# First norm of a two-layer mixer kernel: turned in chunks of two tiles, its gain applied as columns

## The chip, the cores and the metric

One core of one Trainium2 chip. The metric is the device time of one execution in microseconds, the median of several runs. TensorE multiplies and turns (transposes), VectorE (DVE in the rows), ScalarE (ACT) and GpSimd (POOL) compute, SyncE (SP) issues most DMAs. All data is fp32.

## The reference

Two layers of three mixers (difference attention, latent attention, cross attention to a memory), each followed by a two-matrix MLP, and then a third block of another kind. Only the first lines matter here; `x` is 512 rows by 1024 columns:

```python
def rmsnorm(x, gain):
    y = x * lax.rsqrt(jnp.mean(x * x, axis=-1, keepdims=True) + EPS)
    return y * gain
for l in range(DEPTH):
    h = rmsnorm(x, g_mix[l])
    dq, dk, dv, c_q, c_kv_kr, xq, gate_logits = jnp.split(h @ w_in[l], split_idx, axis=-1)
```

The program computes `c_q` (384 columns) first and `c_kv_kr` (288 columns) second, then the others.

## The kernel before, in words

Rows are cut into four tiles of 128 (t = 0 to 3), the 1024 columns of `h` into eight chunks of 128 (k = 0 to 7). For a product the rows of `h` are turned, so that each chunk lies on the partitions: `h_T_hi` and `h_T_lo` hold the turned `h` as a high part in the rounded matmul format and the rest. Weights are split in the same way: a unit of 256 weight rows (two chunks) is loaded by a DMA of SyncE, ScalarE writes the high part (L361, "weights_high_r"), VectorE the low part (L368, "weights_r"). Every product is three matmuls: high by high (L427), high by low (L428), low by high (L429).

Each engine runs its own list in order, and a wait in the list holds everything behind it. The lists are made by a planner: each stage gets times in units of one step of the products (`P_.at`, `P_.beside`), and each engine takes the steps of all stages in order of these times, at equal times in order of entry. TensorE can have a later time for a step than the others (the third entry of `at`).

The first section, cq, has four units of weights and two passes, tiles 0 and 1 and then tiles 2 and 3: a step is one unit by one tile, six matmuls of 384 columns. So cq is plan times 0 to 15, and ckv, matmuls of 288 columns, is 16 to 31. `Tokens.act` and `Tokens.dve` split the weights ahead of use: at cq's step 0 up to the fourth unit, at 2 the fifth, at 4 the sixth. Six units fit in the weight buffer.

The first norm is `StartNorm` (L894). Before: the vector g_mix is loaded broadcast over all partitions (512 KB, SyncE), the squares (L934, ScalarE) wait for the identity too, VectorE multiplies x by the gain (L990), takes the inverse roots of two tiles' sums (`Root`, L703 to L720) and scales tile 0 (L972), ScalarE scales tile 1 (L956). TensorE turns both (L919, 16 turns of 128x128), ScalarE copies out the high part (L942, 512 columns at a time) and VectorE the low part (L980). Tiles 2 and 3 follow with one operation for scale and gain (L1010). The first weight loads wait until x tile 1 has landed (`sp.wait_ge("x_in", 1)`). All four high parts and all four low parts of tiles 0 and 1 come before the first product.

Around it stand the tables of sines and cosines: `TableTurns` (L1654 to L1667, the whole turns), `TableRest` (L1686 to L1695) and `TableSines` (L1712 on ScalarE, L1723 on VectorE), then `Gains` (L1740 to L1767, scaling of small vectors), and `LatentNorm` of cq (squares L1178, scaling L1193), whose turned rows (L632) are used later. cq and ckv are written to a ring of two PSUM banks ("gemm 2": banks 0 and 1) and copied out by ScalarE (L581).

Of the kernel before, what the change touches and what calls it, by code (L numbers as in the profile page):

```python
# [15 lines left out]
P = 128  # L16
# [369 lines left out]
class Tokens(Stage):  # L386
# [3 lines left out]
    def __init__(self, c, tag, xT, chunks, src, sink, ready=(), tiles=NT, ring="gemm", together=NT, tile_ready=lambda t: ()):  # L390
        self.c, self.tag, self.xT, self.chunks, self.sink, self.ready, self.tiles = c, tag, xT, chunks, sink, ready, tiles
        self.ring, self.cols, self.tile_ready = ring, src.shape[1], tile_ready
# [11 lines left out]
    def pe(self):  # L404
# [489 lines left out]
class StartNorm(TileNorm):  # L894


    n = 6
# [4 lines left out]
    def tile_scaled(self, t, g, lane):  # L902
        self.c.values[("scaled", self.tag, t, g)] = lane.end

    def sp(self):
        sp = self.c.sp
        sp.wait_ge("x_in", 1)
        self.c.stream.sp(0)
        for _ in range(self.n):
            yield  # L910

    def pe_turn(self, t):
        c, pe = self.c, self.c.pe
        for g in range(2):
            pe.wait_ge("scaled", self.tag, t, g)
            bank = c.fill(self.tag, t, g, ring=self.ring)
            for k in range(4):
                at = (4 * g + k) * P
                mm = pe.e.transpose(bank[:, k * P:(k + 1) * P], self.xg[:, t, at:at + P], c.ident[:, :])  # L919
            mm.then_inc(*pe.tell("filled", self.tag, t, g))  # L920

    def pe(self):
        for pair in ((), (), (0, 1), (), (2,), (3,)):
            for t in pair:
                self.pe_turn(t)
            yield
# [10 lines left out]
    def act_high(self, t):  # L937
        c, ac = self.c, self.c.ac
        for g in range(2):
            ac.wait_ge("filled", self.tag, t, g)  # L940
            ac.wait_all(self.free)
            ac.e.activation(self.tile(c.hT_all[0], t, g), self.got(t, g), ACT.Copy).then_inc(*ac.tell("turned_high", self.tag, t, g))  # L942

    def act(self):
# [3 lines left out]
        for t in range(2):  # L948
            self.act_squares(t)
        yield  # L950
        c.stream.act(1)
        for g in range(2):
            xg = self.halves(self.xg[:, 1, :])[g]
            ac.wait_ge("gained", self.tag, 1, g)
            ac.wait_ge("inverse_root", self.roots[0].tag)
            ac.e.activation(xg, xg, ACT.Copy, scale=self.sums[0][:, 1:2]).then_inc(*ac.tell("scaled_act", self.tag, g))  # L956
            self.tile_scaled(1, g, ac)
        yield
        for t in range(2):
            self.act_high(t)  # L960
        for t in range(2, NT):
            self.act_squares(t)
        yield
        yield
        for t in range(2, NT):
            self.act_high(t)
            yield

    def dve_scale(self, t, g):
        ve, xg = self.c.ve, self.halves(self.xg[:, t, :])[g]  # L970
        ve.wait_ge("gained", self.tag, t, g)
        ve.e.tensor_scalar(xg, xg, self.sums[0][:, t:t + 1], None, ALU.mult).then_inc(*ve.tell("scaled_dve", self.tag, t, g))  # L972
        self.tile_scaled(t, g, ve)

    def dve_low(self, t):
        c, ve = self.c, self.c.ve
        for g in range(2):
            ve.wait_ge("turned_high", self.tag, t, g)
            ve.wait_all(self.free)
            ve.e.tensor_tensor(self.tile(c.hT_all[1], t, g), self.got(t, g), self.tile(c.hT_all[0], t, g).bitcast(F32),  # L980
                               ALU.subtract).then_inc(*ve.frees(self.tag, t, g))

    def dve(self):
        c, ve = self.c, self.c.ve
        ve.wait_all(self.gain_in)
        for t in range(2):
            for h in range(2):
                x, gain, xg = (self.halves(y)[h] for y in (c.x[:, t, :], self.gain, self.xg[:, t, :]))
                ve.wait_all(self.x_ready(t, h))
                ve.e.tensor_tensor(xg, x, gain, ALU.mult).then_inc(*ve.tell("gained", self.tag, t, h))  # L990
        for h in range(2):
            ve.wait_ge("tile_squares", self.tag, 1, h)
        self.roots[0].dve()
        for g in range(2):
            self.dve_scale(0, g)
        yield
        c.stream.dve(1)
        yield
        for t in range(2):
            self.dve_low(t)  # L1000
        c.stream.dve(3)
        yield
        for h in range(2):
            ve.wait_ge("tile_squares", self.tag, NT - 1, h)
        self.roots[2].dve()
        for t in range(2, NT):
            for g in range(2):
                x, gain, xg = (self.halves(y)[g] for y in (c.x[:, t, :], self.gain, self.xg[:, t, :]))
                ve.wait_all(self.x_ready(t, g))
                ve.e.scalar_tensor_tensor(xg, x, self.sums[0][:, t:t + 1], gain, ALU.mult, ALU.mult).then_inc(*ve.tell("gained", self.tag, t, g))  # L1010
                self.tile_scaled(t, g, ve)
        yield
        for t in range(2, NT):
            self.dve_low(t)
            yield

# [627 lines left out]
class TableTurns(Stage):  # L1644
# [7 lines left out]
    def dve(self):  # L1652
        c, ve, t_ = self.t.c, self.t.c.ve, self.t
        ve.e.memset(c.stat[:, 0:1], 0.0).then_inc(*ve.tell("zero"))  # L1654
# [125 lines left out]
class Layer1:  # L1780
# [3 lines left out]
    def __init__(self, c, l, plan, start, x_marks, hT_free, norm_times):  # L1784
# [44 lines left out]
        if l == 0:  # L1829
            tables = Tables(c, ((self.cos_d, self.sin_d), (self.cos_r, self.sin_r)), [("in", "positions")])  # L1830
            P_.at(Load(c, "identity", [(c.ident[:, :], i["identity"])], []), (-2.9,))
            P_.at(Load(c, "positions", [(c.pos_i[:, :], i["positions"]),
                                        (tables.freq, i["inv_freq"][0, :].partition_broadcast(P))], [], True), (-3,))
        norm_cells = wide_norm_cells(c)
        gain_load = Load(c, tag("g_mix"), [(norm_cells[0], i["g_mix"][l].partition_broadcast(P))], hT_free if l else [])
        P_.at(gain_load, (norm_times[0][0] - 1,))
        norm_of = (c, tag("norm"), x_marks, norm_cells[0], [("in", tag("g_mix"))], *norm_cells[1:], wide(A, NT), hT_free, hT_free)
# [4 lines left out]
        def section(name, dst, col, n, free, ring="gemm 2"):  # L1842
            return Tokens(c, tag(name), c.hT, KD, w[:, col:col + n], CopyOut(c, lambda t: dst[t][:, 0:n], free, by="act"),
                          ring=ring, together=2, tile_ready=norm.done)
# [8 lines left out]
        cq_job, ckv_job = section("cq", cq, C_CQ, MQ, x_gone), section("ckv", ckv, C_CKV, MKV + MR, x_gone)  # L1853
# [2294 lines left out]
class Program:  # L4148


    def __init__(self, c, out):
        self.c = c
        self.plan = plan = Plan()
        both = lambda t, h: [("x_in", t), ("in", "identity")]
        start, hT_free, x_marks = [], [("in", "identity")], both
        for l in range(DEPTH):
            plan.begin()
            times = (tile_times(-16, 4, 4.8),) if l else ((-0.9, -0.8, -0.7, 0.1, 5.8, 5.9),)
# [27 lines left out]
def build(nc, ins, out):  # L4186
# [30 lines left out]
    c.pos_i = sb("positions_int", [P, NT], I32)  # L4217
# [56 lines left out]
def laid_out(inputs):  # L4274
    packed = [name for name, n in (*ROWS_1, *COLUMNS_1, *ROWS_2, *COLUMNS_2)]
    arrays = {name: a for name, a in inputs.items() if name not in packed}
    arrays["positions"] = inputs["positions"].reshape(NT, P).T
    arrays["vectors_1"] = np.stack([vectors(inputs, l, ROWS_1, COLUMNS_1) for l in range(DEPTH)])
# [15 lines left out]
```

## Time and profile before

| what | value |
|---|---|
| median of 3 runs | 3432.21 us (3430.88 to 3433.6) |
| the profiled execution | 3431.43 us |
| its span | 3429.9 us |
| mean granted clock of TensorE | 0.992 |
| TensorE busy | 3310.9 us, 97% |
| VectorE, ScalarE busy | 2018.7 us (59%), 1354.2 us (39%) |

The span is the time between the first and the last record of the profile; 1.5 us of the execution lie around it. The granted clock is 1.00 for 2.4 GHz and 0.50 for 1.2 GHz.

### The profile page before, as it was taken

Reading aid. Unit: us, or ns where it says so; the run is one execution under the profiler, and the core shown is the slowest. Engines: PE = TensorE matmul, PEld = TensorE weight load, DVE = VectorE, ACT = ScalarE, POOL = GpSimd, SP = SyncE. Lnnn points to the kernel's source line nnn. Section 1 sums busy time; section 2 is a strip of 40 time slices with the busy share of each in tenths; the row PEclk is TensorE's granted clock in tenths of the full one; section 3 lists DMA queues with packets and bytes.
Section 4 is the critical chain, followed back from the end, with each engine's and each line's share of the span. In section 5 each row is a group of like instructions: output and inputs, shape, how many; then the busy total and the mean of one; then the engine's idle time right before and its main releaser. Section 6 shows DMA issues by size and latency. Waiting matters only on the chain.

```text
span 3429.9 us, 53077 instructions
## 1 busy us (share of the span) xinstructions
PE 3310.9 (97%) x21864; PEld 2720.9 (79%) x21864; DVE 2018.7 (59%) x3803; ACT 1354.2 (39%) x2604; POOL 0.2 (0%) x4
## 2 busy tenths in 40 slices
PE   7989999999999999999999999999999999999998
PEld 7777788888888777788888888777777788888887
DVE  6776753554436776753554438775766678664434
ACT  5456543342225466543343224434443324232222
POOL 0000000000000000000000000000000000000000
PEclk9999999999999999999999999999999999999999
DMA  4221223233324221223233334333411235433332
GB/s 141 80 70 50 56 74 105 92 99 98 98 99 127 86 64 50 57 79 105 86 105 99 96 101 118 89 92 106 125 38 40 92 95 157 135 97 94 97 98 86
DMA packets 353875, 315.31 MB, mean 92 GB/s; under 512 B 10288, under 2 KB 281776, under 8 KB 353636
## 3 DMA queue, kind: packets, MB, share of 16 engines
q1 hardware_dynamic: 352916, 309.75, 29.9%
q8 instruction: 175, 2.87, 0.3%
q10 hardware_dynamic: 720, 2.16, 0.2%
q14 instruction: 64, 0.52, 0.0%
HBM read 288.28 MB, written 23.59 MB: 91 GB/s over the span
## 4 chain that ended last, share of the span: by engine, by line
PE 80%; DVE 11%; ACT 5%; issue 3%; DMA 2%; SPq 0%; DVEq 0%; ACTq 0%
PE banks L532 14%; PE banks L534 13%; PE banks L533 13%; PE banks L427 8%; PE banks L429 8%; PE banks L428 8%; DVE weights_r L368 2%; PE banks L632 1%; ACT weights_high_r L361 1%; PE banks L2928 1%; PE banks L2867 1%; PE banks L1241 1%; PE banks L1228 1%; PE banks L1332 1%; PE banks L2881 1%
## 5 line engine op out<-in xcount | busy, mean ns | idle before, releaser
L368 DVE TENSOR_TENSOR weights_r<-weights,weights_high_r 128x1024 fp32r<-128x1024 f32 (+2 forms) x517 | 592.9, 1154 | 355.7 <-ACT weights_high_r L361 354.6
L532 PE MATMUL banks<-h_T_hi,weights_high_r 128*128 128x512 f32 (+2 forms) x1912 | 759.6, 397 | 10.6 <-DVE h_T_lo L881 4.7
L534 PE MATMUL banks<-h_T_hi,weights_r 128*128 128x512 f32 (+2 forms) x1912 | 737.9, 386 | 0.0
L533 PE MATMUL banks<-h_T_lo,weights_high_r 128*128 128x512 f32 (+2 forms) x1912 | 737.5, 386 | 0.0
L361 ACT ACTIVATE weights_high_r<-weights 128x1024 fp32r<-128x1024 f32 (+2 forms) x517 | 511.2, 1000 | 360.8 <-DMA weights<-in_w_mlp 213.3
L532 PEld LDWEIGHTS banks<-h_T_hi,weights_high_r 128*128 128x128 f32 x1912 | 361.4, 189 | 98.6 <-issue 28.8
L534 PEld LDWEIGHTS banks<-h_T_hi,weights_r 128*128 128x128 f32 x1912 | 361.2, 189 | 72.7
L533 PEld LDWEIGHTS banks<-h_T_lo,weights_high_r 128*128 128x128 f32 x1912 | 361.7, 189 | 68.0 <-issue 2.6
L427 PE MATMUL banks<-weights_high_r,h_T_hi 128*128 128x512 f32 (+2 forms) x672 | 279.3, 416 | 9.2 <-DVE gate L2208 3.7
L429 PE MATMUL banks<-weights_high_r,h_T_lo 128*128 128x512 f32 (+2 forms) x672 | 254.9, 379 | 0.0
L428 PE MATMUL banks<-weights_r,h_T_hi 128*128 128x512 f32 (+2 forms) x672 | 254.7, 379 | 0.0
L602 DVE TENSOR_TENSOR cellsX<-cellsX,banks 128x512 f32<-128x512 f32 x112 | 76.7, 685 | 276.3 <-PE banks L429 276.2
L427 PE MATMUL banks<-weights_high_r,cellsM_r 128*128 128x512 f32 (+1 forms) x464 | 181.6, 391 | 0.0
L428 PE MATMUL banks<-weights_r,cellsM_r 128*128 128x512 f32 (+1 forms) x464 | 178.1, 384 | 0.0
L429 PE MATMUL banks<-weights_high_r,cellsC_r 128*128 128x512 f32 x432 | 169.2, 392 | 0.0
L427 PEld LDWEIGHTS banks<-weights_high_r,h_T_hi 128*128 128x128 f32 x672 | 127.6, 190 | 41.3 <-issue 9.7
L427 PE MATMUL banks<-weights_high_r,cellsE_r 128*128 128x512 f32 x384 | 150.3, 391 | 2.4 <-DVE cellsS L3898 2.4
L428 PE MATMUL banks<-weights_r,cellsE_r 128*128 128x512 f32 x384 | 150.0, 391 | 0.0
L429 PE MATMUL banks<-weights_high_r,cellsB_r 128*128 128x512 f32 x384 | 149.6, 390 | 0.0
L428 PEld LDWEIGHTS banks<-weights_r,h_T_hi 128*128 128x128 f32 x672 | 128.0, 190 | 23.2 <-issue 3.9
L429 PEld LDWEIGHTS banks<-weights_high_r,h_T_lo 128*128 128x128 f32 x672 | 127.5, 190 | 22.9
L1541 DVE TENSOR_TENSOR gate<-gate,banks 128x512 f32<-128x512 f32 x64 | 44.0, 687 | 131.2 <-ACT gate L1533 131.2
(562 smaller groups left out, 5228.5 us busy)
## 6 DMA issues: line engine op xcount, KB each, us to landing
weights<-in_w_in SPq DMA_DIRECT2D x183, 512.0 KB, 3.8
weights<-in_w_mlp SPq DMA_DIRECT2D x128, 512.0 KB, 3.8
weights<-in_ffn_w_in SPq DMA_DIRECT2D x44, 512.0 KB, 3.8
weights<-in_w_out SPq DMA_DIRECT2D x24, 512.0 KB, 3.6
weights<-in_ffn_w_down SPq DMA_DIRECT2D x22, 512.0 KB, 3.5
weights<-in_w_mem_kv SPq DMA_DIRECT2D x16, 512.0 KB, 3.5
weights<-in_w_diff_o SPq DMA_DIRECT2D x16, 512.0 KB, 3.6
weights<-in_w_mla_o SPq DMA_DIRECT2D x8, 512.0 KB, 3.4
```

The costliest lines, as they stand in the source:

```text
L361: ac.e.activation(self.part(c.w_high_r, u), self.part(c.w_raw, u), ACT.Copy).then_inc(*ac.tell("high", u))
L368: ve.e.tensor_tensor(self.part(c.w_raw_r, u), self.part(c.w_raw, u), self.part(c.w_high_r, u).bitcast(F32), ALU.subtract).then_inc(*ve.tel ...
L427: pe.e.matmul(out, lhsT=hi[k][:, tok], rhs=wh[:, j, :], start=(k == 0), stop=False)
L428: pe.e.matmul(out, lhsT=hi[k][:, tok], rhs=wl[:, j, :], start=False, stop=False)
L429: mm = pe.e.matmul(out, lhsT=lo[k][:, tok], rhs=wh[:, j, :], start=False, stop=last)
L532: pe.e.matmul(out, lhsT=wh[:, k, :], rhs=hi[k][:, cols], start=(k == 0), stop=False)
L533: pe.e.matmul(out, lhsT=wh[:, k, :], rhs=lo[k][:, cols], start=False, stop=False)
L534: mm = pe.e.matmul(out, lhsT=wl[:, k, :], rhs=hi[k][:, cols], start=False, stop=(k == self.chunks - 1))
L602: ve.e.tensor_tensor(dst, dst, got, ALU.add).then_inc(*ve.frees(*key))
L632: mm = pe.e.transpose(bank[0:m, at:at + rows], src, c.ident[0:rows, 0:rows])
L1228: mm = pe.e.matmul(bank[:, 0:v[j].shape[-1]], lhsT=c.pT[n % 2][:, j * P:(j + 1) * P], rhs=v[j], start=(j == 0), stop=(j == len(v) - 1))
L1541: ve.e.tensor_tensor(y, y, got, ALU.mult).then_inc(*ve.frees(*key))
```

## The change

The vector arrives as eight columns (128 partitions by 8) instead of a broadcast row, and is multiplied in after the turn, in the copies out of PSUM, where a chunk's columns of `h` lie on the partitions. The identity is the first load of SyncE's queue and the columns the second; the six first weight loads follow at once, and then positions and frequencies, vectors and mem. x tiles still come on ScalarE's queue. The squares no longer wait for the identity. After the turn of two chunks of two tiles (a bank), the first product may start: `chunk_ready` is a new wait of `Tokens`. Between its wait for the identity and its wait for the scaled rows TensorE turns the identity 28 times into the first bank. cq and ckv of the first layer use the ring of four banks. The tables and the gains have later times.

```diff
 class Tokens(Stage):
             if first:
                 pe.wait_ge("low", u)
+                for k in range(part):
+                    pe.wait_all(self.chunk_ready(n, k0[u] + k))
 class StartNorm(TileNorm):
     def sp(self):
-        sp.wait_ge("x_in", 1)
         self.c.stream.sp(0)
+    def pe_turn(self, pair, b):
+        first = pair == b == 0
+        if first:
+            bank = c.fill(self.tag, pair, b, ring=self.ring)
+            for _ in range(28):
+                pe.e.transpose(bank[:, 0:P], c.ident[:, :], c.ident[:, :])
+        for t in (2 * pair, 2 * pair + 1):
+            pe.wait_ge("scaled", self.tag, t, b // 2)
+        if not first:
+            bank = c.fill(self.tag, pair, b, ring=self.ring)
+        for k in range(2):
+            at = (2 * b + k) * P
+            for t in range(2):
+                mm = pe.e.transpose(bank[:, (2 * k + t) * P:(2 * k + t + 1) * P], self.xg[:, 2 * pair + t, at:at + P], c.ident[:, :])
+        mm.then_inc(*pe.tell("filled", self.tag, pair, b))
     def pe(self):
-        for pair in ((), (), (0, 1), (), (2,), (3,)):
+        self.c.pe.wait_ge("in", "identity")
+        for pair in range(2):
+            for b in range(4):
+                self.pe_turn(pair, b)
+                yield
+    def act_high(self, pair, b):
+        for k in range(2):
+            f = 2 * b + k
+            ac.e.activation(c.hT[0][f][:, self.cols(pair)], self.got(pair, b, k), ACT.Copy, scale=c.first_gain[:, f:f + 1])
     def act(self):
         for t in range(2):
             self.act_squares(t)
         c.stream.act(1)
+        self.act_scale(1)
+        self.act_high(0, 0)
+        c.stream.act(2)
+        yield
+        self.act_high(0, 1)
+        self.act_squares(2)
+        c.stream.act(3)
+        self.act_squares(3)
+        yield
+        self.act_high(0, 2)
+        c.stream.act(4)
+        yield
+        self.act_high(0, 3)
+        self.act_scale(3)
+        yield
+        for b in range(4):
+            self.act_high(1, b)
+            yield
+    def dve_low(self, pair, b):
+        for k in range(2):
+            f = 2 * b + k
+            ve.e.scalar_tensor_tensor(c.hT[1][f][:, self.cols(pair)], self.got(pair, b, k), c.first_gain[:, f:f + 1],
+                                      c.hT[0][f][:, self.cols(pair)].bitcast(F32), ALU.mult, ALU.subtract)
     def dve(self):
-                ve.e.tensor_tensor(xg, x, gain, ALU.mult)
+        ve.e.memset(c.stat[:, 0:1], 0.0)
+        self.dve_root(0)
+        self.dve_scale(0)
+        c.stream.dve(1)
+        self.dve_low(0, 0)
+        yield
+        for b in range(1, 4):
+            c.stream.dve(b + 1)
+            if b == 2:
+                self.dve_root(2)
+            self.dve_low(0, b)
+            if b == 2:
+                self.dve_scale(2)
+            yield
+        for b in range(4):
+            self.dve_low(1, b)
+            yield
+    def chunk_done(self, pair, k):
+        return [("emptied", self.tag, pair, k // 2)]
 class Layer1:
+            P_.at(Load(c, "first columns", [(c.first_gain, i["g_mix_columns"])], []), (-2.8,))
-            P_.at(Load(c, "positions", ...), (-3,))
+            P_.at(Load(c, "positions", ...), (0.5,))
-        cq_job, ckv_job = section("cq", ...), section("ckv", ...)
+        cq_job, ckv_job = section("cq", ..., "gemm 2" if l else "gemm", **({} if l else {"chunk_ready": norm.chunk_done})), section("ckv", ..., "gemm 2" if l else "gemm")
-            P_.at(tables.whole, (-1.5,))
-            P_.at(tables.rest, (6.2,))
-            P_.at(tables.sines, (11.6, 13.6))
-        P_.beside(Gains(c, l, self, vectors_in), 15, 18)
+            P_.at(tables.whole, (5.7,))
+            P_.at(tables.rest, (7.8,))
+            P_.at(tables.sines, (16.3, 16.6))
+        P_.beside(Gains(c, l, self, vectors_in), 15 if l else 17.5, 18 if l else 20.5)
 class Program:
-            times = ... ((-0.9, -0.8, -0.7, 0.1, 5.8, 5.9),)
+            times = ... ((-0.9, -0.8, 1.5, 3.5, 5.5, 5.6, 7.6, 7.7), [0, 0, 0, 0, 0.9, 1, 1.9, 3.8])
```

`act_scale` is the scaling that L956 did, straight from x and for tiles 1 and 3; `dve_scale` the same on VectorE for tiles 0 and 2; `dve_root` waits for the squares of two tiles and takes their inverse roots. The numbers in `times` are the plan times of the norm's eight steps, the list behind them what TensorE's are later by.

## Rows read from the trace of the kernel before

**Rows 1.** The page: the chain that ended last, by engine.

```profile
PE 80%; DVE 11%; ACT 5%; issue 3%; DMA 2%; SPq 0%; DVEq 0%; ACTq 0%
```

**Rows 2.** Waits of TensorE, whole span: us in total, times, longest.

```profile
PE banks L919 <- DVE cellsA L972: 17.6, 1, 17.6
PE banks L427 <- DVE weights_r L368: 1.9, 1, 1.9
```

**Rows 3.** Timeline until the first turn: start us, us, engine, line, what [idle before].

```profile
8.13 3.06 SPq L381 DMA_DIRECT2D weights<-in_w_in  x6
9.29 0.63 ACT L934 ACTIVATE cellsS<-cellsX 128x512 f32<-128x512 f32 x1 [4.15 <-DMA identity<-in_identity]
12.44 2.50 DVE L990 TENSOR_TENSOR cellsA<-cellsX,cellsS 128x512 f32<-128x512 f32 x4 [2.29 <-DMA cellsS<-in_g_mix]
13.78 0.84 ACT L361 ACTIVATE weights_high_r<-weights 128x768 fp32r<-128x768 f32 x1 [1.93 <-DMA weights<-in_w_in]
15.07 0.16 DVE L703 TENSOR_TENSOR tile_sums<-tile_sums 128x2 f32<-128x2 f32 x1
17.05 0.88 DVE L972 TENSOR_SCALAR cellsA<-cellsA,tile_sums 128x512 f32<-128x512 f32 x2
17.11 1.34 ACT L956 ACTIVATE cellsA<-cellsA,tile_sums 128x512 f32<-128x512 f32 x2 [2.48 <-DVE tile_sums L720]
17.59 3.68 PE L919 MATMUL banks<-identity,cellsA 128*128 128x128 f32 x16 [17.59 <-DVE cellsA L972]
```

**Rows 4.** DMA issues in stretches 0.7:0.75, 1.16:1.18, 8.1:8.2: KB, us to landing.

```profile
cellsX<-in_x ACTq DMA_DIRECT2D x1, 512.0 KB, 4.1
positions_int<-in_positions SPq DMA_DIRECT2D x1, 2.0 KB, 3.3
...
cellsX<-in_x ACTq DMA_DIRECT2D x1, 512.0 KB, 7.0
...
weights<-in_w_in SPq DMA_DIRECT2D x1, 384.0 KB, 5.6
```

**Rows 5.** Busy time by stretch: PE, PEld, DVE, ACT, POOL, clock, DMA share, GB/s.

```profile
0.00:10.00 10.00, 0.00 (x0) 0.00 (x0) 2.63 (x10) 2.20 (x5) 0.20 (x4) 1.00 0.70 235
10.00:17.50 7.50, 0.00 (x0) 0.00 (x0) 4.73 (x17) 3.08 (x9) 0.00 (x0) 1.00 1.06 383
26.00:32.00 6.00, 5.87 (x25) 5.84 (x26) 5.52 (x17) 1.70 (x3) 0.00 (x0) 0.72 0.00 1
```

**Rows 6.** Timeline of the first sections, all engines.

```profile
23.00 0.33 PE L427 MATMUL banks<-weights_high_r,h_T_hi 128*128 128x384 f32 x1
26.13 0.61 PE L427 MATMUL banks<-weights_high_r,h_T_hi 128*128 128x384 f32 x1 [1.90 <-DVE weights_r L368]
31.99 1.91 PE L919 MATMUL banks<-identity,cellsA 128*128 128x128 f32 x16
33.66 0.42 PE L427 MATMUL banks<-weights_high_r,h_T_hi 128*128 128x384 f32 x1
36.43 0.96 DVE L1686 SCALAR_TENSOR_TENSOR probabilities<-probabilities 128x768 f32<-128x768 f32 x1
40.20 0.56 DVE L1695 TENSOR_SCALAR probabilities<-probabilities 128x768 f32<-128x768 f32 x1
44.15 0.29 PE L427 MATMUL banks<-weights_high_r,h_T_hi 128*128 128x288 f32 x1
53.62 1.41 DVE L1193 TENSOR_SCALAR cellsX<-cellsX,small 128x384 f32<-128x384 f32 x4
55.17 0.63 PE L632 MATMUL banks<-identity,cellsX 128*128 128x128 f32 x4 [0.22 <-DVE cellsX L1193]
```

**Rows 7.** Groups by line and form in 0:60: busy us, mean ns.

```profile
L368 DVE TENSOR_TENSOR weights_r<-weights,weights_high_r 128x768 fp32r<-128x768 f32 x4 | 3.6, 952 | 2.5 <-ACT weights_high_r L361 2.5
L643 ACT ACTIVATE cellsM_r<-banks,small 128x512 fp32r<-128x512 f32 x3 | 2.1, 687 | 4.9 <-PE banks L632 4.9
L1767 DVE TENSOR_TENSOR small<-small 128x256 f32<-128x256 f32 x2 | 0.8, 418 | 0.0
```

More of the change, by code:

```diff
@@ L386, with __init__ @@
 class Tokens(Stage):
-    def __init__(self, c, tag, xT, chunks, src, sink, ready=(), tiles=NT, ring="gemm", together=NT, tile_ready=lambda t: ()):
+    def __init__(self, c, tag, xT, chunks, src, sink, ready=(), tiles=NT, ring="gemm", together=NT, tile_ready=lambda t: (), chunk_ready=lambda n, k: ()):
         self.c, self.tag, self.xT, self.chunks, self.sink, self.ready, self.tiles = c, tag, xT, chunks, sink, ready, tiles
+        self.chunk_ready = chunk_ready
         self.ring, self.cols, self.tile_ready = ring, src.shape[1], tile_ready
@@ L894 @@
 class StartNorm(TileNorm):
-    n = 6
+    n = 8
     def __init__(self, c, tag, *args):
         super().__init__(c, tag, *args, pairs=True)
-    def tile_scaled(self, t, g, lane):
-        self.c.values[("scaled", self.tag, t, g)] = lane.end
     def sp(self):
-        sp = self.c.sp
-        sp.wait_ge("x_in", 1)
         self.c.stream.sp(0)
@@ L910, in sp, with cols, got @@
             yield
-    def pe_turn(self, t):
-        c, pe = self.c, self.c.pe
[L914 to L920, printed above, removed]
-    def pe(self):
-        for pair in ((), (), (0, 1), (), (2,), (3,)):
-            for t in pair:
-                self.pe_turn(t)
-            yield
+    def cols(self, pair):
+        return slice(2 * pair * P, 2 * (pair + 1) * P)
+    def got(self, pair, b, k):
+        return self.c.slots[(self.tag, pair, b)][:, k * 2 * P:(k + 1) * 2 * P]
+    def pe_turn(self, pair, b):
+        c, pe = self.c, self.c.pe
+        first = pair == b == 0
[12 more added lines that the diff above has]
+        mm.then_inc(*pe.tell("filled", self.tag, pair, b))
+    def pe(self):
+        self.c.pe.wait_ge("in", "identity")
[3 more added lines that the diff above has]
+                yield
     def act_squares(self, t):
@@ L935, in act_squares, with act_scale @@
                             accum_out=self.sums[h][:, t:t + 1]).then_inc(*ac.tell("tile_squares", self.tag, t, h))
-    def act_high(self, t):
+    def act_scale(self, t):
         c, ac = self.c, self.c.ac
+        ac.wait_ge("inverse_root", self.roots[t - 1].tag)
         for g in range(2):
-            ac.wait_ge("filled", self.tag, t, g)
-            ac.wait_all(self.free)
-            ac.e.activation(self.tile(c.hT_all[0], t, g), self.got(t, g), ACT.Copy).then_inc(*ac.tell("turned_high", self.tag, t, g))
+            ac.e.activation(self.halves(self.xg[:, t, :])[g], self.halves(c.x[:, t, :])[g], ACT.Copy,
+                            scale=self.sums[0][:, t:t + 1]).then_inc(*ac.tell("scaled_act", self.tag, t, g))
+            c.values[("scaled", self.tag, t, g)] = ac.end
+    def act_high(self, pair, b):
+        c, ac = self.c, self.c.ac
+        ac.wait_ge("filled", self.tag, pair, b)
+        ac.wait_all(self.gain_in)
+        ac.wait_all(self.free)
+        for k in range(2):
+            f = 2 * b + k
+            ac.e.activation(c.hT[0][f][:, self.cols(pair)], self.got(pair, b, k), ACT.Copy, scale=c.first_gain[:, f:f + 1]).then_inc(
+                *(ac.tell("turned_high", self.tag, pair, b) if k else ac.step()))
     def act(self):
@@ L949, in act @@
             self.act_squares(t)
+        c.stream.act(1)
+        self.act_scale(1)
+        self.act_high(0, 0)
+        c.stream.act(2)
         yield
[L951 to L957, printed above, removed]
+        self.act_high(0, 1)
@@ L975, in dve_low, with dve_scale @@
-    def dve_low(self, t):
+    def dve_scale(self, t):
         c, ve = self.c, self.c.ve
         for g in range(2):
[L978 to L981, printed above, removed]
+            ve.e.tensor_scalar(self.halves(self.xg[:, t, :])[g], self.halves(c.x[:, t, :])[g], self.sums[0][:, t:t + 1], None,
+                               ALU.mult).then_inc(*ve.tell("scaled_dve", self.tag, t, g))
+            c.values[("scaled", self.tag, t, g)] = ve.end
@@ L983, in dve, with dve_root @@
+    def dve_root(self, t):
+        ve = self.c.ve
+        for h in range(2):
+            ve.wait_ge("tile_squares", self.tag, t + 1, h)
+        self.roots[t].dve()
     def dve(self):
         c, ve = self.c, self.c.ve
[L985 to L995, printed above, removed]
-        yield
[L997 to L1011, printed above, removed]
@@ L1018, with done, x_gone @@
+        for b in range(4):
[3 more added lines that the diff above has]
+        return [("emptied", self.tag, pair, k // 2)]
+    def done(self, t=None):
+        return [("emptied", self.tag, pair, b) for pair in (range(2) if t is None else (t // 2,)) for b in range(4)]
+    def x_gone(self):
+        return [("tile_squares", self.tag, NT - 1, 1), ("scaled", self.tag, NT - 1, 1), ("scaled", self.tag, NT - 2, 1)]
 class FinalNorm(Stage):
```

48 lines of the change are left out of this document (22 added, 26 removed).

## The prediction

> **What bounds the kernel.** I read the page first: the chain that ended last is TensorE for 80% [rows 1]. So the end moves by what TensorE gains or loses, and only where it stands still or runs slowly. The waits of TensorE come second: one of them, 17.6 us until the first turned rows, is more than twice any other, and the change goes for it; the 1.9 us until the second unit of weights lies in the same stretch [rows 2]. Third, the timeline says what made up the 17.6 us [rows 3]. The squares stood until the identity was there (9.29). The multiply by the gain stood until the broadcast vector was there (12.44) and four of them took 2.5 us. Then came the root, 15.07 to 17.05, the scaling, and the first turn at 17.59. Fourth, from there to ckv's first product at 44.15 [rows 6] are 26.6 us. They hold 96 products of cq, which go at 0.173 us when fast (60 of them lie between 33.66 and 44.15, 10.5 us), and 32 turns at 0.115 us (16 in 1.9): 16.6 + 3.7 = 20.3 us. The other 6.3 us are low clock and the 1.9 us wait. All that can be had is therefore some 6 us there and some 6 us of the 17.6.
>
> **Part 1, the start.** Times are from the start of the profiled span.
>
> x tile 1 landed at 1.17 + 7.0 = 8.2 [rows 4]. The gain broadcast, positions and frequencies no longer share the engines ahead of it, but weights do. Bounds are 7.2 and 9.4 (the last if weights take half of the 2.35 MB that had moved by 10 us [rows 5]); I take 7.8, near the row. Its squares: eight halves and roots are paced 0.61 us, so two take 1.3 (9.29 to about 11.9 for four [rows 3]): 9.1. Root 2.0 us: 11.1. VectorE scales tile 0 by 12.0 (0.88 for two).
>
> ScalarE however has the first unit of weights between the squares and the scaling of tile 1. That unit landed at 8.13 + 5.6 = 13.7 [rows 4]. Its issue no longer waits for x tile 1 and falls at about 1.6. Before it or beside it go x (2.1 MB), the unit (0.39) and identity and columns (0.07), together 2.56 MB; 2.35 MB had moved by 10 us and the rate was then 0.383 MB per us [rows 5], so it lands at 10.6. Bounds: 9.0 (if x3 comes after it) and 13.7 as before. Split 0.84, first half of tile 1 scaled in 0.67 (1.34 for two) [rows 3]: first turn of rows at **12.2**, for 17.59, with bounds 11.7 (root) and 15.3.
>
> The 28 turns of the identity go on TensorE ahead of that. Positions, as first of SyncE's queue, landed at 4.0 and x tile 0 at 4.8 [rows 4], so I take 4.5 for the identity. At the slow pace, 0.23 us each (16 in 3.68 [rows 3]), they take 6.4 us and end at 10.9; at 0.115 they take 3.2. They cost nothing while they end before 12.2.
>
> **Part 2, cq.** Prices first. A high part of two chunks is two ScalarE operations of 256 columns with a scale. The row of that kind has 512 columns and 0.69 us [rows 7]; 256 must lie between half of it and all of it, I take 0.40 each and 0.72 for a pair at pace. A low part is two VectorE operations of 256, of which a plain one is 0.42 [rows 7]: 0.85 for a pair (0.7 to 1.5). The unit's split is 0.75 on ScalarE at pace and 0.95 on VectorE.
>
> ScalarE, in list order from 12.95 (first bank filled): high 0, unit 2, high 1, two squares 1.25, unit 3, two squares 1.25, unit 4, then high 2: it starts at 19.0. VectorE: low 0 at 13.7, over at 14.5; low 1 over at 16.2; then units 3 and 4, the last until 20.0 as it waits for ScalarE; then the root of tiles 2 and 3, 2.0 us; then low 2, over at **22.8**. TensorE: first two banks, stands from 13.2 to 14.5, 12 products to 16.6, third bank, 12 products to 19.1, fourth bank to 19.6, and then it stands **3.2 us** for low 2. This wait takes the place of the old 1.9 us one; queued behind the root on VectorE are low 2, the scaling of tile 2 and both later low parts, and TensorE waits for each. After it the clock is at its lower level for 3.4 us (after the 1.9 us wait the stretch 26 to 32 had a mean of 0.72, that is 0.28 x 6 / 0.5 [rows 5]), which costs some 1.6 us, partly hidden. From 22.8: unit 3 to 26.4, then one step, two banks, one step to 29.4, low part of pair 1 at 29.7, then 48 products 8.3 and two banks 0.9: ckv starts at **38.9**, for 44.15, so 5.2 us earlier. If TensorE comes slowly out of the start, the 3.2 us wait shrinks by as much; that term hardly moves (4.8 to 6.2 with the clock low or high at each place).
>
> Four banks for two: the copies of a pass no longer stand before the next. The rows show 10.49 us for what 60 products at 0.173 do in 10.38 [rows 6], so 0.1 us at most for cq. I take 0.
>
> **Part 3, what is late next.** The rest of the tables took VectorE from 36.43 to 40.76, ahead of ckv, and it then had idle time. Now it stands behind the last low part, which TensorE fills only after two units of the second pass: over about 2.3 us before ckv, so the tables' rest (4.35 us) ends 2.1 us after ckv's start. From there to the scaled cq rows VectorE has units 0.7 + 0.7, sines 0.45, the two parts of Gains 0.9 + 1.7, two units 2.4, the root 1.8, the scaling 1.4 (53.62 to 55.03 [rows 6]), with gaps 10.4 us: ready 12.6 us after ckv's start. TensorE wanted them 10.8 us after it (55.17 less the 0.22 wait [rows 6], less 44.15). So it stands 1.8 us where it stood 0.2: **1.6 us lost**. Whether the clock falls there too is open; one chance in three at 1.6 us, in the sum as 0.4. The whole tables (2.9 us) lie between low 1 and low 2 of pair 1, while TensorE does 12 products; hidden. Later times and orders are as before, VectorE idles 1.5 us and more behind that point, and everything moves by the same amount.
>
> Sum: 5.2 - 1.6 - 0.4 = 3.2; the other way round of the clock in the first stretch adds 0.3 on average: **3.5 us**. The profiled execution is 3431.4 (span 3429.9), so 3427.9 against it; the median is 0.8 above the profiled one. Prediction 3428.7.
>
> **A rule that speaks against it.** At 17.59 the turns go at 0.23 us and products follow at the slow pace until 23.0, which is 3.5 us of turns and 1.7 us of products; after the wait at 26.13 products alone ran slowly for 3.4 us [rows 3, 5, 6]. So here turns seem to have counted towards the rise of the clock. The Trainium skill, page "TensorE: Matmul & The Clock Gate", Part 4 on PE-mode transpose, says that turns do not count as busy for the clock. By it the 28 turns would buy nothing; this trace speaks rather against it but has no stretch of turns alone.
>
> **Rivals.**
> 1. The identity's turns warm nothing, so the change does not do what it says there. Then banks 0 and 1 take 0.46 us longer each and the first 12 products run at 0.32 for 0.173, 2.7 us in all; the wait for low 2 takes up most of it, as VectorE's list moves only by 0.5. Gain 3.0 us: 3429.2. For it: no rows of turns alone. Chance 0.25, in the same class as the forecast.
> 2. Faster: the rise holds and there is no wait at low 2 (VectorE's root comes early enough as ScalarE runs ahead of my list). Then ckv starts at 14.5 + 16.6 + 2.8 = 33.9, 10.2 us earlier, less 1.7 at the cq turns: 8.5 us, 3423.7. Against it: five ScalarE operations and a root in the list order that I counted from rows. With the parts between (no fall of the clock at either wait, an earlier unit of weights) 0.2 for more than 6.9 us.
> 3. Slower: the filler stands in the way. TensorE's list is in order. If the identity lands where it did before, at 9.2 (its squares waited for it until 9.29 [rows 3]), 28 slow turns end at 15.7, rows begin 3.5 us later and the gain to ckv is 1.7. With 1.6 lost at the cq turns and 1.6 of clock there the end is 1.5 us later: 3433.7. It decides from an identity at 5.8 on. Against it: now it is first in its queue. Chance 0.1; over 0.2% slower would need 5 us more.
> 4. VectorE is the bound to the cq turns and the gain is given back there, since its list holds 2 us more than TensorE's time. Gain 0 to 1.5: 3431.5. Chance 0.15.
>
> **Numbers.** Forecast 0.3, rivals 0.25, 0.2, 0.1, 0.15. A measurement of this kernel can tell about 0.2% from no change, 6.9 us, so most cases are "same". Faster 0.2, same 0.78, slower 0.02. The range 3423.5 to 3433 takes in rival 2 at its end and most of rival 3, with the bounds of the unit's landing (3 us).
>
> **What would show it.** Right: first row turn near 12.2; a wait of TensorE for the low part of the third bank near 3 us; ckv's first product near 39; the first cq turn near 51.6 with a wait of 1 to 2 us. Wrong: no wait at the third bank; the identity's turns still running when rows are scaled; rows' turns at 0.115 us from the start with products fast at once, or at 0.23 us after 28 turns (rival 1); a ckv start under 36 or over 42.

## The result, and the profile after

The changed kernel is slower: 3445.6 us median (10 runs, 3439.6 to 3451.1) against 3437.0 before (10 runs, 3430.9 to 3443.4), ratio 1.0028, interval 1.0018 to 1.0037. Forecast was 3428.7 in a range of 3423.5 to 3433. In a second comparison on another occasion the ratio was 1.0022 (1.0013 to 1.0031). The three runs of before known at the time lay in the lower half of its spread. Single executions of the unchanged kernel differ by more than the loss (3430.9 to 3443.4 in these ten), so all that follows goes by medians, intervals, and stretches of the trace.

The start went as foreseen, and better up to ckv. The page of the profile (the chain that ended last) and the timeline of the changed kernel, columns as in [rows 3]:

```profile
PE 80%; DVE 10%; ACT 5%; issue 3%; DMA 1%; SPq 0%; DVEq 0%; ACTq 0%
...
4.07 5.37 PE L922 MATMUL banks<-identity 128*128 128x128 f32 x28 [4.07 <-DMA identity<-in_identity]
5.90 0.63 ACT L946 ACTIVATE cellsS<-cellsX 128x512 f32<-128x512 f32 x1
9.25 0.84 ACT L361 ACTIVATE weights_high_r<-weights 128x768 fp32r<-128x768 f32 x1 [2.02 <-DMA weights<-in_w_in]
10.85 1.06 PE L930 MATMUL banks<-identity,cellsA 128*128 128x128 f32 x8 [1.41 <-ACT cellsA L953]
13.41 0.41 PE L430 MATMUL banks<-weights_high_r,h_T_hi 128*128 128x384 f32 x1 [1.50 <-DVE h_T_lo L1007]
21.85 0.48 PE L430 MATMUL banks<-weights_high_r,h_T_hi 128*128 128x384 f32 x1 [3.14 <-DVE h_T_lo L1007]
22.13 0.52 PE L431 MATMUL banks<-weights_r,h_T_hi 128*128 128x384 f32 x1
38.48 0.29 PE L430 MATMUL banks<-weights_high_r,h_T_hi 128*128 128x288 f32 x1
52.14 0.63 PE L635 MATMUL banks<-identity,cellsX 128*128 128x128 f32 x4 [3.11 <-DVE cellsX L1224]
```

The first turn of rows is at 10.85 (17.59 before), ckv starts at 38.5 (44.15), the first cq turn is at 52.1 (55.2) [rows 3, 6]. The clock falls behind the waits of 3.14 and 3.11 us. What is left at 60 us is 1.5 us. The waits of TensorE in the first 200 us, us in total, times, longest:

```profile
PE banks L430 <- DVE h_T_lo L1007: 5.0, 3, 3.1
PE banks L922 <- DMA identity<-in_identity: 4.1, 1, 4.1
PE banks L635 <- DVE cellsX L1224: 3.1, 1, 3.1
```

So the loss is behind. To find it I took the 517 low parts of weights on VectorE (L368), which come in the same order in every one of these kernels, as milestones: part 11 (59 us) starts 1.5 us earlier than before, part 29 (173 us) 1.5 earlier, part 53 (366 us) 2.5 later, part 341 (2053 us) 1.1 later, part 353 (2141 us) 6.0 later, part 389 (2455 us) 6.5 later, part 413 (2805 us) 13.5 later, the last 13.6 later. Two stretches carry most of it, 4.9 and 7.0 us. The 4 us between parts 29 and 53 are low clock at 176 and 288 us; the kernel before had low clock there too in its second profile, so this stretch tells nothing of the change. In 2053 to 2141 us both kernels do the same work, but the clock is low in one of them; busy time by stretch, columns as in [rows 5], before and then after:

```profile
2088.00:2102.00 14.00, 14.00 (x88) 12.29 (x88) 10.13 (x17) 4.32 (x6) 0.00 (x0) 1.00 0.39 109
```

```profile
2088.00:2102.00 14.00, 12.86 (x60) 12.13 (x61) 7.53 (x16) 2.66 (x4) 0.00 (x0) 0.63 0.27 75
```

And in 2455 to 2805, the third block's recurrence with thousands of short products, TensorE stops with nothing in the profile that it waits for (the profile puts such time down to "issue"). The waits in that stretch, before (2455:2800) and after (2455:2810):

```profile
PE banks L2867 <- issue: 3.0, 5, 1.1
PE banks L2893 <- issue: 0.3, 1, 0.3
```

```profile
PE banks L2899 <- issue: 5.1, 8, 0.8
PE banks L2960 <- issue: 3.1, 3, 2.5
```

3.3 us of such stops became 8.2. I call this stretch R below: the time from low part 389 to 413, 350.3 us before and 357.3 after. Where its clock was low, half of that time is taken off as loss ("net"): 346.9 and 352.2. A second profile of each kernel gave 348.6 and 353.3, so the change adds 4 to 6 us net.

### The profile page after: what moved, and what is told of

Same layout as the page of the kernel before. It is cut to its first block, busy times and chain, and to the rows that moved or that the text cites. A ratio compares the mean times of both kernels' runs of the same rounds, so it can differ in the third digit from the quotient of the medians.

```text
span 3443.5 us, 53150 instructions
## 1 busy us (share of the span) xinstructions
PE 3328.0 (97%) x21892; PEld 2736.3 (79%) x21892; DVE 2017.1 (59%) x3805; ACT 1355.2 (39%) x2614; POOL 0.2 (0%) x4
## 4 chain that ended last, share of the span: by engine, by line
PE 80%; DVE 10%; ACT 5%; issue 3%; DMA 1%; SPq 0%; DVEq 0%; ACTq 0%
PE banks L535 14%; PE banks L536 13%; PE banks L537 13%; PE banks L430 9%; PE banks L432 8%; PE banks L431 8%; DVE weights_r L368 1%; PE banks L635 1%; ACT weights_high_r L361 1%; PE banks L2899 1%; PE banks L2960 1%; PE banks L1259 1%; PE banks L1272 1%; PE banks L1363 1%; PE banks L2913 1%
## 5 line engine op out<-in xcount | busy, mean ns | idle before, releaser
L368 DVE TENSOR_TENSOR weights_r<-weights,weights_high_r 128x1024 fp32r<-128x1024 f32 (+2 forms) x517 | 593.5, 1155 | 355.8 <-ACT weights_high_r L361 354.8
L535 PE MATMUL banks<-h_T_hi,weights_high_r 128*128 128x512 f32 (+2 forms) x1912 | 761.9, 398 | 10.6 <-DVE h_T_lo L884 4.7
```

Of the source, the lines that this page charges most:

```text
L368: ve.e.tensor_tensor(self.part(c.w_raw_r, u), self.part(c.w_raw, u), self.part(c.w_high_r, u).bitcast(F32), ALU.subtract).then_inc(*ve.tel ...
L535: pe.e.matmul(out, lhsT=wh[:, k, :], rhs=hi[k][:, cols], start=(k == 0), stop=False)
```

## The experiments

Three theories stand behind the expectations. **E**, early activity of TensorE changes how the clock falls later; **F**, it is the 56 more instructions (28 turns, each a weight load and a matmul) that stand in TensorE's list ahead of R. A third, **A**, that the pattern falls by chance, was tested first. Each version below has one profile; every median is of 10 to 12 runs, of 7 for turns_42. Behind a median stand the ratio to the kernel before, run beside it, and the 95% interval. The ratio is estimated from all runs and need not be the quotient of the two medians. The median of the kernel before was 3436.5 beside the first four versions, 3436.9 beside turns_at_cq, turns_14, turns_42 and tables_early, 3433.7 beside turns_late, wide_early and sines_early, and 3436.5 beside before_with_wide, before_turns_again, sines_early_again and sines_early_wide.

**before_again, after_again**, no edit.

> The kernel before, unchanged, as a yardstick: is the 8.7 us by which the changed kernel is slower a property of the two programs, or do the low-clock stretches behind the changed part fall differently in every execution? Theory A (they fall by chance in each execution): ratio 1.000 within 0.1%, and its profile shows low-clock stretches at other places than 1200, 1310, 2173, 2248 us and so on. Theory B (the pattern belongs to the program): ratio 1.000, the same places, low clock for some 53 us in all, mean clock 0.992.

> The changed kernel, unchanged. Theory A: the mean clock lies between 0.988 and 0.992 and its time is within 0.1% of the kernel before, since its first 170 us are 1.5 us shorter. Theory B: slower by 8 to 9 us again (1.0026), clock 0.988, low clock at 175, 288, 1452 and 2090 us again, where TensorE waits 1.1 to 1.8 us in both programs.

Before: 3436.0 (1.0002, 0.9992 to 1.0013). After: 3443.7 (1.0022, 1.0013 to 1.0031). The low-clock stretches of the kernel before came at other places this time (178 and 288 us among them, none at 26), 53 us in all again, so part of the pattern is chance; the difference between the programs is not. A falls as the reason, and B is only half right.

**no_turns**

```diff
-            for _ in range(28):
-                pe.e.transpose(bank[:, 0:P], c.ident[:, :], c.ident[:, :])
```

> The changed kernel without the 28 turns of the identity. If the early activity of TensorE is what sets how the later falls of the clock come (theory B with the turns as cause), the time goes back to that of the kernel before or under it: 0.999 to 1.000. If the turns only warm the clock for cq, the first product's start stays at 13.4 us, the first 24 products go slowly, the wait of 3.1 us for the third bank shrinks to about 1, and the time stays 1.0025 within 0.05%.

3436.3 (1.0002, 0.9993 to 1.0010): without the turns the whole loss is gone. R takes 348.5 us with no low clock in it, stops 3.1 us. The first cq turn still waits 3.1 us. What the turns did locally is seen in its timeline:

```profile
11.29 1.94 PE L928 MATMUL banks<-identity,cellsA 128*128 128x128 f32 x8 [11.29 <-ACT cellsA L951]
14.31 0.66 PE L430 MATMUL banks<-weights_high_r,h_T_hi 128*128 128x384 f32 x1 [1.08 <-DVE h_T_lo L1005]
14.77 0.52 PE L431 MATMUL banks<-weights_r,h_T_hi 128*128 128x384 f32 x1
```

Eight turns take 1.94 us where they took 1.06, and the products go at 0.32 us each where they went at 0.17. (The granted clock reads 1.00 here from 11 to 17 us all the same. Its first entry in this trace is at 18.1 us, when the products turn fast, so ahead of it the level is read from the pace.) At 60 us the kernel is no later for it (low part 11 at 57.3, where it was at 57.8), since the wait for the third bank shrinks from 3.1 to 1.4 us.

**before_with_turns**, the 28 turns put into the kernel before:

```diff
+            if t == g == 0:
+                pe.wait_ge("in", "identity")
+                bank = c.fill(self.tag, t, g, ring=self.ring)
+                for _ in range(28):
+                    pe.e.transpose(bank[:, 0:P], c.ident[:, :], c.ident[:, :])
             pe.wait_ge("scaled", self.tag, t, g)
```

> The kernel before with the 28 turns of the identity between its landing (9.2 us) and the first scaled rows (17.6 us), nothing else. They end by 15. If early activity of TensorE sets the later falls: slower by 5 to 10 us though the first 60 us are the same or shorter. If not: the turns at 17.6 and the products behind them run faster, at most 2.4 us of gain up to 26 us, most of it lost in the wait for the second unit of weights; ratio 0.9995 to 1.000.

3442.8 (1.0018, 1.0008 to 1.0028): the turns alone make the kernel before 6 us slower. E and F both allow that.

**turns_at_cq**: no turns at the start, 28 in the wait for the first cq turn (`Turn.pe_one`, ahead of `pe.wait_all(self.ready)`).

> The changed kernel with its 28 turns of the identity moved from the start into the wait of 3.1 us before the first cq turn. Theory F (fetch: what costs is that 28 turns more stand in TensorE's instruction list ahead of the third block's recurrence, so that its stops for the next instructions fall at other places): the stretch from 2455 us to 2805 us, which took 350.3 before, 357.3 and 355.1 after and 348.5 without turns, takes 355 or more again, and the median is 3441 or more. Theory E (early activity of TensorE changes how the clock falls later): that stretch takes 348 to 351, the median 3435 to 3437.

3441.4 (1.0015, 1.0005 to 1.0024), and R takes 358.6 (net 353.5), with these stops:

```profile
PE banks L2903 <- issue: 6.0, 8, 1.1
PE banks L2964 <- issue: 2.3, 1, 2.3
```

There is no early activity here, and R is as long as with it, so E is out for this stretch. The local use of the turns was good: low part 11 at 55.5, 2.3 us better than the changed kernel, no low clock up to 60 us. It is given back in R.

**turns_14, turns_42**: 14 and 42 instead of 28.

> The changed kernel with 14 turns of the identity instead of 28. Theory F: the stops lie between those of no turns and of 28, so the stretch takes anything from 348 to 357 us, with the issue waits of TensorE at other lines than in both; theory E: as with none or half of the 7.4 us, median 3436 to 3441.

> The changed kernel with 42 turns of the identity. They end near 11.5 us at the rate of the 28 (5.4 us from 4.1), so they hardly delay the rows. Theory E: more early activity, so slower than the changed kernel or like it, 3443 or more. Theory F: no order with the number of turns; if 42 shift the stops on into a place that is hidden, the time can come back to 3437.

14: 3438.0 (1.0002, 0.9992 to 1.0013), R 350.7, net 347.3, stops 3.8 us. 42: 3448.5 (1.0036, 1.0023 to 1.0050), R 360.1, net 356.7, stops 11.1 us:

```profile
PE banks L2899 <- issue: 9.6, 13, 1.2
PE banks L430 <- issue: 0.8, 1, 0.8
PE banks L535 <- issue: 0.7, 1, 0.7
```

Over 0, 14, 28 and 42 turns the stops go 3.1, 3.8, 8.2, 11.1. E would have such an order; F had said none, but allows it.

**turns_late, wide_early**: the 28 turns behind R (in the turn of the last norm); and at the start, in place of them,

```diff
+            for _ in range(4):
+                pe.e.matmul(bank[:, :], lhsT=c.ident[:, :], rhs=c.ident[:, :].unsqueeze(1).broadcast_to([P, 4, P]), start=True, stop=True)
```

> The changed kernel with its 28 turns of the identity moved behind the third block's recurrence, to the first turn of the norm ahead of the last two products. The same instructions in the same program, but none of them ahead of the recurrence. Theory F: the stretch that took 350.3 us before and 357.3 after takes 348 to 350 as without turns; the median is that of no turns (3436.3) plus the turns' own time of at most 3.2 us, so 3436 to 3440. Theory E says the same here as for the run without turns; what it would not allow is that the run with turns at the first cq turns was slow. If the stretch takes 355 us here too, F falls: then 56 more instructions cost wherever they stand.

> The changed kernel with 4 products of the identity with itself repeated, 512 columns each, in place of the 28 turns: early activity of TensorE with 8 more instructions in its list in place of 56. Theory F: the stretch of the recurrence takes 348 to 351 us, median 3436 to 3438. Theory E: slow like the changed kernel, 3442 to 3446.

Late: 3438.7 (1.0006, 0.9997 to 1.0016), R 351.4 where 348 to 350 was expected, net 349.7, stops 4.3 us; the 2.4 us over no turns are within the turns' own 3.2. Wide: 3436.6 (1.0004, 0.9994 to 1.0013), R 348.7, stops 3.7 us, though TensorE is busy from 4.2 to 10.7:

```profile
4.22 6.43 PE L922 MATMUL banks<-identity 128*128 128x512 f32 x8 [4.22 <-DMA identity<-in_identity]
11.10 1.07 PE L930 MATMUL banks<-identity,cellsA 128*128 128x128 f32 x8 [0.45 <-ACT cellsA L953]
```

The profile shows each of the four as two. Early activity without many instructions costs nothing measurable, and many instructions without early activity cost (turns_at_cq). F holds for R. Its stops in the wide kernel, for comparison with the above:

```profile
PE banks L2960 <- issue: 3.1, 7, 0.8
PE banks L2925 <- issue: 0.6, 1, 0.6
```

The traces say where the stops fall. Number TensorE's records (weight loads, products and its semaphore instructions) in order of start. In the kernel before the stops come 512, 3585, 1791, 1792 and 1792 records apart, in the changed one 1025, 1792, 1791, 513, 255, 1024, 1793, 767, 1024 and 1793: multiples of 256, within one. Over all 17 profiles there are 143 such stops, and each stands at a number that leaves 193 or 194 when divided by 256. So the places where TensorE can stop are fixed in its list, every 256 records, and the 56 instructions of the turns push other instructions of R onto them. R begins at record 23811 in no_turns, turns_late, tables_early and both profiles of sines_early: stops 3.1 to 4.5 us, net 348.2 to 349.9. It begins at 23867 in both profiles of the changed kernel and in turns_at_cq: stops 8.2 to 8.4 us, net 352.2 to 353.5. The two groups don't overlap, so R's share of the loss is 2 to 5 us.

**before_with_wide, before_turns_again**: the same contrast in the kernel before.

> The kernel before with 4 products of the identity, 512 columns each, between its landing and the first scaled rows, in place of the 28 turns that made it 6 us slower. Theory F: as the kernel before, ratio 0.999 to 1.0005. If early activity costs in this kernel in spite of F: slower by 5 us or more again.

> The kernel before with 28 turns, unchanged, for a second profile. It was 6 us slower while the stretch of the recurrence took only 351.0 us in its profile (350.3 and 348.6 before). Theory F: the median is 3440 or more again and that stretch takes 351 to 355 with issue waits over 4 us in all. If the stretch is under 350 and the time still 3442, something else than the stops in the recurrence costs here.

Wide: 3435.9 (1.0002, 0.9993 to 1.0012). Turns: 3442.3 (1.0012, 1.0003 to 1.0022). So here too it is the many instructions that cost, and not activity alone. But in both kernels with turns R took 351.0 us, net 349.3 and 347.6, with 5.3 and 5.0 us of stops and not the 8 of the changed kernel, though R begins at record 23862, only five earlier. Stops of 1.7 us more than before come with next to no net loss in R. The loss lies in two other stretches, both times the same: 2053 to 2141 us took 94.9 and 94.8, where the kernel before took 87.9 and 87.5 and the one with wide products 88.2, and 2805 to 2974 took 172.7 and 172.5 (169.2 and 171.4). In the first of them the clock is low:

```profile
2088.00:2102.00 14.00, 13.40 (x57) 12.66 (x58) 6.74 (x14) 2.66 (x4) 0.00 (x0) 0.54 0.27 75
```

The changed kernel without turns had low clock there as well (92.5 us for the whole), and so had every other variant, only not the kernel before (two profiles) and the kernel before with wide products. What decides it is open. There is a wait of TensorE of 1 to 2 us at 2088 in all of them, and products of 128 columns behind it. It is the clock alone: with half of the low time taken off, 2053 to 2141 us takes 86.7 to 88.2 us in all 17 profiles, and 2805 to 2974 us takes 167 to 168.

How much of the loss is the clock can be read from the runs, since each has its span and mean granted clock. Span times (1 - clock) is the most that low clock can have cost, half of the time spent at the lower level; that it is near the real cost is seen in 2053 to 2141 us. The rest is the span without it. Means, as the difference from the kernel before run beside it, in us (standard errors some 1.4 and 0.8):

| version | low clock | rest |
|---|---|---|
| changed kernel, second comparison | +8.4 | -1.0 |
| no_turns | +2.5 | -2.6 |
| turns_at_cq | +3.2 | +2.0 |
| turns_14 | +4.6 | -3.4 |
| turns_42 | +6.5 | +5.8 |
| turns_late | +3.4 | +0.2 |
| wide_early | +4.3 | -2.7 |
| kernel before with turns, twice | +6.4, +5.0 | -0.4, -0.7 |
| kernel before with wide | +1.9 | -2.6 |

With the turns at cq the rest fits F: it is 4.6 us more than in no_turns, and R is 5 us longer net. But in the changed kernel the turns add only 1.6 us of rest and up to 5.9 us of low clock, and in the kernel before low clock is all that they add. So the larger part of the loss goes through the clock, and the stops of F alone don't account for it. It comes with 28 turns at the start, and less or not at all with wide products there or with the turns at cq or behind R. For the clock E is therefore not out; why turns should do it and wide products less, no run shows.

**tables_early, sines_early**, both without turns. The wait of 3.1 us before the first cq turn was to go:

```diff
-            P_.at(tables.whole, (5.7,))
-            P_.at(tables.rest, (7.8,))
-            P_.at(tables.sines, (16.3, 16.6))
-        P_.beside(Gains(c, l, self, vectors_in), 15 if l else 17.5, 18 if l else 20.5)
+            P_.at(tables.whole, (5.45,))
+            P_.at(tables.rest, (5.65,))
+            P_.at(tables.sines, (8.2, 8.7))
+        P_.beside(Gains(c, l, self, vectors_in), 15 if l else 7.9, 18 if l else 9.9)
```

tables_early has the first two lines of it, sines_early all four.

> The changed kernel without turns, the whole turns of the tables ahead of the first low part of tiles 2 and 3, and their rest directly behind the second, where VectorE was idle for 3.5 and 1.6 us. The 3.1 us wait before the first cq turn should go, as VectorE no longer has the rest (4.3 us) between the last low part and ckv's weights; at most 1 us of it comes back as a wait for the low part of the third bank. First 60 us: 3 to 4 us shorter than without turns (57.3), and no low clock at 52 us; median 3431.5 to 3434. If the cq turns wait for something else (ScalarE's copies), it stays 3436.

> As tables_early, and the sines and the gains behind the last high and low part of tiles 2 and 3, where ScalarE and VectorE were idle for 3.2 and 3.4 us before ckv. In tables_early ScalarE loaded two tables (1.28 us each) and waited 0.85 us between ckv's start and the squares of cq, and the wait for the first cq turn stayed 3.1 us. If this is what was late, that wait goes to under 1 us, the first 60 us take 54 to 56 (58.1 with tables_early), and the median is 3430 to 3433. If VectorE's own list (weights, root, scaling) is what is late, the wait stays over 2 us.

tables_early: 3433.7 (0.9999, 0.9989 to 1.0009). Its expectation was wrong: the wait stayed 3.10 us, though VectorE had the tables' rest behind it at 33.9 us. ScalarE's timeline says what was late:

```profile
40.33 1.28 ACT L1740 ACT_TABLE_LOAD   x1
43.72 1.28 ACT L1768 ACT_TABLE_LOAD   x1
45.85 0.20 ACT L1768 ACTIVATE small<-small 128x2 f32<-128x2 f32 x1 [0.85 <-DVE small L1781]
49.13 0.19 ACT L1207 ACTIVATION_READ_ACCUMULATOR cellsS<-cellsX 128x1 f32 x1
```

Two table loads, the sines and a wait stand ahead of cq's squares; the last square ends at 49.3, and the root (1.8) and scaling (1.4) follow. In the changed kernel the two loads stand at 39.8 and 43.2, and the squares end at 48.8. sines_early puts sines and gains where ScalarE was idle, with the tables' rest early as well: 3429.2 (0.9990, 0.9979 to 1.0000), and the wait is gone.

**sines_early_again, sines_early_wide** (the latter with the four wide products).

> The version that came out fastest (3429.2 against 3433.7 before in the same call, interval 0.9979 to 1.0000), once more: 0.9985 to 0.9995 if it is really 3 to 5 us faster.

> The fastest version with the 4 wide products of the identity at the start. The first 12 products of cq go fast, but they then wait longer for the low part of the third bank: the first 60 us shrink by 0 to 1 us against 53.9, median 3428 to 3430.

Again: 3433.3 (0.9993, 0.9984 to 1.0002). Wide: 3433.8 (0.9990, 0.9979 to 1.0000), low part 11 at 54.8 where it was at 53.6, so warming buys nothing. The waits of sines_early_again up to 62 us, and its turns at cq:

```profile
PE banks L928 <- ACT cellsA L951: 11.0, 1, 11.0
PE banks L430 <- DVE h_T_lo L1005: 3.5, 4, 1.1
...
49.54 0.60 PE L635 MATMUL banks<-identity,cellsX 128*128 128x128 f32 x4
50.77 0.60 PE L635 MATMUL banks<-identity,cellsX 128*128 128x128 f32 x4
```

Locally this is 5 us less than before (low part 11 at 53.9 and 53.6 for 59.3 and 58.6). The two comparisons gave 4.6 and 3.2 us against the kernel before run beside them (3433.7 and 3436.5). Each interval touches 1, so it is faster than the changed kernel beyond doubt and likely 3 to 5 us faster than before, under what one comparison of this kernel can settle. Split as in the table, low clock is +1.2 and +1.4 and the rest -5.0 and -5.2: the local gain is there to the end.

## Why the prediction was wrong

- **Part 1, right, its landings too late.** Forecasts stand in brackets. The identity landed at 4.1 (4.5), the 28 turns ended at 9.4 (10.9), x tile 1 landed at 5.9 (7.8) and its squares ran without a wait, the unit of weights was there at 9.25 (10.6), the first turn of rows at 10.85 (12.2). The weights beside it did not hold x back.
- **Part 2, right, in part by luck.** The wait for the third bank was forecast at 3.2 us until 22.8, measured 3.14 until 21.85; low clock behind it as forecast; ckv at 38.5 for 38.9. In the second profile the clock fell earlier, at 13.9, the wait was 1.6 us, and no fall came behind it; how the 3.2 us split between wait and clock is not the program's alone.
- **Part 3, mis-sized and with the wrong engine.** The forecast was that TensorE "stands 1.8 us where it stood 0.2"; it stood 3.11. I counted VectorE's list and left out ScalarE's two table loads of 1.28 us and its wait of 0.85. (The part's own sum, 2.1 + 10.4, is 12.5 and not 12.6, which changes nothing.) tables_early showed that VectorE's list was not it. The clock did fall there, which I gave one chance in three. With 2.9 lost for 1.6, and some 1.6 of clock for 0.4, 5.7 us at ckv became 1.5 at 60 us, where the sum said 3.5.
- **The step that failed** is "Later times and orders are as before [...] and everything moves by the same amount". Orders were the same; times were not. With it fell the price of the turns, "They cost nothing while they end before 12.2": they were costed by the time they cover on the array, and not by where they leave the rest of the list nor by what they do to the clock later. Taking them out gave back 7.4 us (3443.7 against 3436.3), and putting them into the kernel before cost it 6. Two things took the term's place. TensorE's stops in R were 8.2 us for 3.3, with R 2 to 5 us longer net than without the turns. And low clock cost up to 39 us of a run in the changed kernel, 33 without the turns and 30 in the kernel before; that larger part has no explanation.
- **Rival 1** (the turns warm nothing) was wrong. In the changed kernel the row turns behind them go at 0.13 us (8 in 1.06) and the products at 13.4 at the full pace, in no_turns the same turns at 0.24 and products at the low level. So turns count. Within the 28 the pace itself changes: 20 turns at 0.21 us, then 8 at 0.11. The rule of the Trainium skill, page "TensorE: Matmul & The Clock Gate", Part 4, by which they do not count, does not hold for these fp32 turns. But the warmth was of no use, as rival 1 said: the wait for low 2 takes it up. And it is not sure: in after_again the clock fell at 13.9, with the same turns.
- **Rival 2** did not happen: there was a wait at low 2. **Rival 4** (the gain given back up to the cq turns, 0 to 1.5 us left) is what the first 60 us did, but through ScalarE's list and not VectorE's.
- **Rival 3** (slower) had the right side and the wrong mechanism: the identity landed at 4.1, not at 9.2. No rival had the loss lie 2000 us behind the edit. That the forecast was so narrow (slower by 0.2%: 0.02) came from summing only the first 60 us.

What stays open: why many turns at the start draw more low clock later; why the low clock at 2090 us comes in nearly all variants and not in the kernel before; and with it why the kernel before with turns loses 6 us where R accounts for little. That the stops are fetches of instructions is inferred (they stand every 256 records or a multiple of it, and the profile has nothing that TensorE waits for), not seen as such. Other numbers than 14, 28 and 42 weren't tried. 128 turns, 256 records, would put R back where it was against the places of the stops; this would test F best, and the order over 14, 28 and 42 may be no more than which instructions met those places.

## What to carry to other kernels

Filler instructions are not free merely because the engine waits there: they shift the engine's whole list, so measure the program with and without them, and if TensorE is to be kept busy use few wide products (here these cost nothing and gained nothing). Look at the "issue" waits of every stretch after an edit at the start, and align both traces by a milestone that all variants have. Split each run into what low clock can have cost and the rest; a gain of 5 us that hides in the spread of the medians shows in the rest. When a wait is predicted on one engine, write out the list of each engine that feeds it, table loads included.

## What the runs showed of the hardware

- TensorE's stops without a visible cause in a stretch of some 7000 short products: 3.3 and 3.6 us before; 3.1, 3.8, 8.2 and 8.4, 11.1 with 0, 14, 28 and 42 extra turns ahead of it in the changed kernel; 5.3 and 5.0 with 28 in the kernel before; 4.3 with 28 behind it; 3.7 with 4 wide products ahead. In each of the 17 profiles, 143 stops in all, any two stand a multiple of 256 TensorE records apart, within one.
- Low clock in a profiled execution of the same program came at different places, 53.5 and 52.9 us in all for the kernel before, 84.8 and 70.8 for the changed one; each execution's time goes with it (kernel before: mean clock 0.993 at 3430 us, 0.989 at 3442).
- Turns of a 128x128 fp32 identity raised the clock by themselves: 28 in 5.4 us from a standing TensorE, 20 at 0.21 us and 8 at 0.11, the row turns behind at 0.13 us each. In the second profile the rise came after 14.
